# Routing on raw rows inside the last projection block of a fused encoder step

## The chip, the cores and the metric

The kernel runs on 1 core of one Trainium2 chip. The metric is the device time of one execution in microseconds; three runs of the kernel before took 517.83, 518.95 and 521.62 us, so the median is 518.95. A core has five engines with queues of their own, which meet only at semaphores: TensorE (PE in the rows, its weight loads PEld), VectorE (DVE), ScalarE (ACT), GpSimd (POOL) and SyncE (SP, which here only issues DMAs). ACT and POOL issue DMAs too.

## The reference, cut to what matters

One layer over 512 prompt tokens and 32 sample tokens of width 1024: norm, one input projection, a gated mixer beside a stick-breaking attention, an output projection with the residual, and then a mixture of experts. The part that the change touches:

```
h = yp + jnp.concatenate([gm, sb], axis=-1) @ w_out[l]
yp = h + hier_moe(rmsnorm(h, norm2_g[l]), *moe_args)

rmsnorm(x, g) = x * rsqrt(mean(x * x) + EPS) * g
lg    = xf @ w_router_group + b_router_group             # 4 group scores
g_sel = argmax(lg)                                       # one group of 4
le    = (xf @ w_router_expert + b_router_expert)[g_sel]  # 4 expert scores of that group
top_v, top_i = top_k(softmax(le), 2)                     # two experts per token
gates = softmax(lg)[g_sel] * top_v / sum(top_v)
y     = sum over the two of gate * (silu(x @ w_gate[e]) * (x @ w_up[e])) @ w_down[e]
```

There are 16 experts of inner width 256. All matrices are float32.

## The kernel before

Tokens are handled in five tiles (NT = 5): four of 128 rows and one of 32, the sample tile, which comes last. `x_sb` holds the rows x, and later h. The projections run as blocks of 512 output columns (`project(blk, after)`, L1469): a block has two halves, each half takes four 128-row pieces of the contraction for all five tiles, and `after[half](t)` puts other TensorE work between two tiles. Full tiles are computed in three float32r passes (L1465 to L1467) from a weight unit that was split in two parts: the high part by ACT, the low part (raw minus high) by DVE or POOL. The sample tile uses plain float32 (L1490). Blocks NB and NB + 1 are the output projection's two halves of columns; the last block, NB + 1, is weight units 12 and 13.

**Between the last projection block and the experts** the order of each queue is written out by hand:

- DVE adds the residual of each finished tile (`add_last`, L1225), normalises it into `xn2` (`norm_h`, L1208), and adds the router's bias (`logits`, L1219).
- ACT squares each finished row half with an accumulated sum (`square_h`, L866), copies transposed rows out of PSUM (`x2T_copy`, L874), and issues the store of normalised rows to the DRAM table `normed_tokens` (`store_normed`, L884).
- POOL makes the inverse root (L579 to L582) and the low part of expert unit 0 in four quarters (L586). The low parts of units 1 and 2 follow in `moe_gathers` (L592 to L596), ahead of the gathers in POOL's queue.
- TensorE transposes the normalised rows (`turn_normed`, L1675) and multiplies them with the padded router weights `wr_pad` (`router`, L1665): eight float32 products of 128 columns per tile. Three tiles' routers come after the projection's end.

The choice then runs on DVE as a chain (L1243 to L1339): in a chain, `link` makes each instruction wait for the one before. It finds the top group, the scores within the group, the two best experts, and the 0/1 selections `sel`. TensorE counts ranks by products with a triangular matrix (L1699 to L1706). A token's rank in its expert is its slot; an expert has CAP = 96 slots in a round. One-hot slot rows (`token_slots`) times token numbers (`slot_table`, L1709) give the token of each slot, which DVE writes to `idx_all`. POOL copies one column of it to `idx_cur` (L609) and issues an indirect DMA which gathers an expert's rows from `normed_tokens` into `xs` (L612). It waits for all stores of normalised rows before.

**The expert stage** (`moe`) takes three weight units of 1 MB per expert. Twelve raw buffers (NRAW) are filled from SP's queue ahead of use: units 0 to 5 once attention is done, unit 6 once unit 11 was used, unit 7 once unit 12 was used, units 8 to 11 once unit 13 was used, that is at the projection's end. Unit m from 12 on waits until units up to m - 12 have both parts made (`raw_free`, L409), and for the landing of the unit two before it (`few_in_flight`, L450). TensorE transposes the gathered rows (L1728), ACT and DVE split them, and the products follow.

After the experts POOL gathers each token's two result rows (L660) and DVE adds them with their gates (L1423).

## Time and profile before

| | |
|---|---|
| Median of three runs | 518.95 us |
| Profiled execution | 517.57 us |
| Its span, first to last instruction | 515.8 us |
| TensorE busy | 445.1 us, 86% |
| VectorE busy | 294.9 us, 57% |
| ScalarE busy | 251.2 us, 49% |
| GpSimd busy | 176.8 us, 34% |
| Mean granted TensorE clock | 0.944 |

The span is what the rows count from; the 1.8 us around it belong to the profiled execution's own time, and this execution is 1.4 us below the median of the runs. Busy shares are averages over stages with different limits, so a change in one stage is read from that stage. Of TensorE's clock 1.00 means 2.4 GHz and 0.50 means 1.2 GHz.

### The profile page before, as it was taken

The numbers are of one execution on the slowest core, as the hardware profiler recorded it, in microseconds if no ns is written. First come the engines' busy times: TensorE is split into PE (matmuls) and PEld (weight loads), VectorE is DVE, ScalarE is ACT, GpSimd is POOL, SyncE is SP. The second block draws the span as 40 slices with busy tenths as digits, with TensorE's granted clock in tenths as the row PEclk, the third lists the DMA queues.
The fourth block names the chain that finished last, engine by engine and source line by source line (L and its number), as shares of the span: only waits on it lengthen the run. The fifth ranks groups of instructions, "written<-read, shape, count | busy, mean of one in ns | idle before, by whom it ended". The sixth has DMA issues, their size and how long they took to land. (4 is left out here: it accounts for less than half of the span.)

```text
span 515.8 us, 7224 instructions
## 1 busy us (share of the span) xinstructions
PE 445.1 (86%) x2569; PEld 329.5 (64%) x2569; DVE 294.9 (57%) x442; ACT 251.2 (49%) x360; POOL 176.8 (34%) x179
## 2 busy tenths in 40 slices
PE   5999999999798999999999941799999999999400
PEld 4877877787586666667777841566666666666200
DVE  3535442354633645562333747358998998998236
ACT  4664333563424636462115521457877877877100
POOL 0384000514200000001003741137767767745270
PEclk9999999999979999999999985789999999999955
DMA  8872222222214000001695695269999999994376
GB/s 254 214 245 84 88 83 81 83 83 102 100 49 169 1 1 1 1 0 42 212 361 175 216 376 183 82 237 326 338 341 304 348 340 340 356 350 169 97 251 268
DMA packets 63445, 94.78 MB, mean 184 GB/s; under 512 B 10592, under 2 KB 43360, under 8 KB 63408
## 3 DMA queue, kind: packets, MB, share of 16 engines
q1 hardware_dynamic: 54336, 69.87, 41.6%
q0 software_dynamic: 5088, 17.89, 10.8%
q10 hardware_dynamic: 3984, 6.56, 3.5%
q8 instruction: 19, 0.31, 0.2%
q14 instruction: 18, 0.15, 0.1%
HBM read 81.27 MB, written 13.04 MB: 183 GB/s over the span
## 5 line engine op out<-in xcount | busy, mean ns | idle before, releaser
L1348 DVE TENSOR_TENSOR wlo<-raw,whi 128x2048 fp32r<-128x2048 f32 (+1 forms) x45 | 96.9, 2154 | 23.1 <-ACT whi L917 23.0
L1465 PE MATMUL bank<-whi,xT_hi 128*128 128x512 f32 x224 | 92.8, 414 | 2.7 <-DVE wlo L1015 2.1
L1466 PE MATMUL bank<-wlo,xT_hi 128*128 128x512 f32 x224 | 89.8, 401 | 0.0
L1467 PE MATMUL bank<-whi,xT_lo 128*128 128x512 f32 x224 | 89.6, 400 | 0.0
L917 ACT ACTIVATE whi<-raw 128x2048 fp32r<-128x2048 f32 x45 | 86.1, 1914 | 5.2 <-PE bank L1467 5.2
L622 POOL TENSOR_TENSOR wlo<-raw,whi 128x1024 fp32r<-128x1024 f32 x16 | 59.7, 3729 | 36.3 <-ACT whi L917 36.3
L1465 PE MATMUL bank<-whi,xsT_hi 128*96 128x512 f32 x128 | 53.8, 420 | 4.7 <-DVE xsT_lo L1354 3.5
L1465 PEld LDWEIGHTS bank<-whi,xT_hi 128*128 128x128 f32 x224 | 42.8, 191 | 14.3 <-issue 3.9
L1466 PE MATMUL bank<-wlo,xsT_hi 128*96 128x512 f32 x128 | 51.5, 403 | 0.0
L1467 PE MATMUL bank<-whi,xsT_lo 128*96 128x512 f32 x128 | 51.3, 401 | 0.0
L1467 PEld LDWEIGHTS bank<-whi,xT_lo 128*128 128x128 f32 x224 | 42.8, 191 | 10.5
L1466 PEld LDWEIGHTS bank<-wlo,xT_hi 128*128 128x128 f32 x224 | 43.0, 192 | 9.0
L1015 DVE SCALAR_TENSOR_TENSOR wlo<-raw,g_col,whi 128x512 fp32r<-128x512 f32 x40 | 27.9, 752 | 29.2 <-ACT whi L694 22.5
L576 POOL MEMSET wr_pad<- 128x1024 f32 x1 | 1.0, 954 | 100.1 <-issue 100.1
L513 POOL TENSOR_SCALAR ssq<-ssq 128x1 f32<-128x1 f32 (+3 forms) x25 | 5.0, 200 | 85.8 <-DVE ssq L1127 65.5
L694 ACT ACTIVATE whi<-raw,g_col 128x512 fp32r<-128x512 f32 x36 | 23.0, 710 | 23.2 <-PE bank L1490 19.5
L1465 PEld LDWEIGHTS bank<-whi,xsT_hi 128*96 128x96 f32 x128 | 21.2, 166 | 18.5 <-issue 7.0
L1465 PE MATMUL bank<-whi,aT_hi 128*96 128x512 f32 x64 | 26.1, 408 | 1.8 <-DVE aT_lo L1364 1.1
L609 POOL COPY idx_cur<-idx_all 96x1 int32<-96x1 int32 (+1 forms) x16 | 20.2, 1260 | 21.7 <-PE bank L1728 11.9
L1467 PEld LDWEIGHTS bank<-whi,xsT_lo 128*96 128x96 f32 x128 | 21.3, 166 | 9.5 <-issue 0.2
L1466 PEld LDWEIGHTS bank<-wlo,xsT_hi 128*96 128x96 f32 x128 | 21.3, 166 | 7.1
L515 POOL TENSOR_TENSOR rstd<-ssq,mhalf 128x1 f32<-128x1 f32 (+3 forms) x25 | 25.1, 1004 | 2.1
(223 smaller groups left out, 774.6 us busy)
## 6 DMA issues: line engine op xcount, KB each, us to landing
raw<-in_w_gate_dram SPq DMA_DIRECT2D x32, 512.0 KB, 6.1
raw<-in_w_up_dram SPq DMA_DIRECT2D x32, 512.0 KB, 7.5
raw<-in_w_down_dram SPq DMA_DIRECT2D x32, 512.0 KB, 6.8
raw<-in_w_in_dram SPq DMA_DIRECT2D x9, 1024.0 KB, 5.2
expert_rows<-yout POOLq DMA_DIRECT2D x16, 384.0 KB, 5.3
raw<-in_w_out_dram SPq DMA_DIRECT2D x4, 1024.0 KB, 5.1
x_sb<-in_x_prompt_dram SPq DMA_DIRECT2D x8, 256.0 KB, 6.1
normed_tokens<-xn ACTq DMA_DIRECT2D x4, 512.0 KB, 2.9
```

The lines of the kernel that those rows point to most:

```text
L513: link(pool.tensor_scalar(s, s, 1.0 / width, EPS, ALU.mult, ALU.add))
L515: return pool.tensor_tensor(dst, s, mhalf[0:s.shape[0], 0:n], ALU.pow)
L576: link(pool.memset(wr_pad[:, :, :], 0.0))
L609: pool.tensor_copy(idx_cur[p][:, :], idx_all[:, bass.ds(i, 1)]).then_inc(idx_cp, 1)
L622: pool.tensor_tensor(wlo[split][:, D:2 * D], eraw[slot][:, D:2 * D], whi[split][:, D:2 * D].bitcast(F32), ALU.subtract).then_inc(m_lo_pool, 1)
L694: ins = act.activation(whi[n % 2][:, c], raw[n % 3][:, c], ACT.Copy, scale=g1_col[:, kk:kk + 1])
L917: act.activation(whi[SPLIT_OF[m3]][:, :], eraw[slot][:, :], ACT.Copy).then_inc(m_hi, 1)
L1015: return dve.scalar_tensor_tensor(out=dst, in0=src, scalar=g1_col[:, kk:kk + 1], in1=hi.bitcast(F32), op0=ALU.mult, op1=ALU.subtract)
L1348: dve.tensor_tensor(wlo[SPLIT_OF[m3]][:, 0:n], eraw[slot][:, 0:n], whi[SPLIT_OF[m3]][:, 0:n].bitcast(F32), ALU.subtract).then_inc(m_lo, 1)
L1465: pe.matmul(acc, x_hi, w_hi, start=start, stop=False)
L1466: pe.matmul(acc, x_hi, w_lo, start=False, stop=False)
L1467: return pe.matmul(acc, x_lo, w_hi, start=False, stop=stop)
```

## The change

1. The router's products are made from the raw rows h, not the normalised ones. The factor 1/rms of a token is applied to the 20 scores afterwards (in `logits`), and the norm's gain is multiplied into the router weights `wr` once, early, by POOL. `wr_pad` goes; the products have 20 columns.
2. Since a raw row half is complete after the block before, the transposes and products of the first 512 columns run in the last block's first half, for all five tiles, and those of the second 512 in its second half. The second half takes the sample tile first (`LAST`), each tile's routing work stands inside the next tile's columns, and that of the last tile follows the projection.
3. POOL multiplies the rows with the gain (`times_g2`), ACT applies 1/rms and stores (`norm_store`). DVE's `norm_h` goes.
4. The expert choice is made over all 16 experts with the other groups pushed down by a large number; `sel` is bf16 and the rank products take the two choices apart. POOL makes the token numbers (`token_ids`). The slot products follow tile by tile behind ten small one-hot instructions, they accumulate both parts of a number, and DVE copies the first two experts' indices from PSUM straight to `idx_cur`.
5. The low parts of units 1 and 2 are made by DVE, the one before and the other after the first tokens' low parts. The places of the results and the gates are worked out after the indices as before. The first product of an expert waits for half of its tokens' parts, not all.
6. Buffers: `xn2` has five buffers, constants of the attention lie in its stack, and padded rows need no masks, since all products run over a tile's own rows.

```diff
+            pool.wait_ge(ld_wr, 16 * (NG + 1))
+            pool.wait_ge(ld_g2c, 16)
+            pool.tensor_tensor(wr[:, :, :], wr[:, :, :],
+                               g2_col[:, :].rearrange("p (k a) -> p k a", a=1).broadcast_to([P, KC, NE]), ALU.mult).then_inc(wr_ok, 1)
             pool.wait_ge(w_ok, 2 * NH)
             pool.wait_ge(pv_ok, NV)
...
+            def times_g2(t, half):
+                c = slice(half * CB, (half + 1) * CB)
+                pool.wait_ge(acc_free[t], 2 + half)
+                pool.tensor_tensor(xn2[t][0:rows[t], c], x_sb[0:rows[t], t, c], g2b[0:rows[t], c], ALU.mult).then_inc(hg_ok, 1)
...
+            for k, t in enumerate(LAST):
+                p = rows[t]
+                times_g2(t, 1)
+                pool.wait_ge(ssq2_ok, NT + k + 1)
+                link(pool.tensor_scalar(ssq[0:p, 3, t:t + 1], ssq[0:p, 3, t:t + 1], 1.0 / D, ssq[0:p, 2, t:t + 1], ALU.mult, ALU.add))
+                pool.tensor_tensor(rstd[0:p, 2, t:t + 1], ssq[0:p, 3, t:t + 1], mhalf[0:p, 0:1], ALU.pow).then_inc(rstd2_ok, 1)
+                if k < 4:
+                    c = slice(k * UNIT // 4, (k + 1) * UNIT // 4)
                     pool.wait_ge(m_hi, 1)
                     ins = pool.tensor_tensor(wlo[SPLIT_OF[0]][:, c], eraw[0][:, c], whi[SPLIT_OF[0]][:, c].bitcast(F32), ALU.subtract)
-                    if t == 3:
+                    if k == 3:
                         ins.then_inc(m_lo, 1)
...
+            pool.wait_ge(sel_ok, 2)
+            for t in range(NT):
+                token_ids(t)
...
-                for m in range(1 if isinstance(r, int) else 0, 3):
-                    pool.wait_ge(m_hi, u0 + m + 1)
...
+                    else:
+                        pool.wait_ge(idx_ok, s + 1)
+                        pool.sem_inc(idx_cp, 1)
                     pool.indirect_dma_start(xs[p][:, :], None, xn_dram[:, :],
...
+            def norm_store(k, t):
+
+                act.wait_ge(hg_ok, NT + k + 1)
+                act.wait_ge(rstd2_ok, k + 1)
+                act.activation(xn2[t][0:rows[t], :], xn2[t][0:rows[t], :], ACT.Copy, scale=rstd[0:rows[t], 2, t:t + 1]).then_inc(xn2_ok, 1)
+                act.wait_ge(xn2_ok, k + 1)
+                act.dma_start(xn_dram[tok(t), :], xn2[t][0:rows[t], :]).then_inc(xn_st, 16)
+
+            for t in range(NT):
+                x2T_copy(t, t, 0)
+                square_h(t, t, 0)
+            first_hi(1, slice(0, 3 * UNIT // 4))
             unit_used(act, U_IN + 2)
...
+            first_hi(0).then_inc(m_hi, 1)
+            first_hi(1, slice(3 * UNIT // 4, UNIT)).then_inc(m_hi, 1)
+            for k, t in enumerate(LAST):
+                square_h(NT + k, t, 1)
+                x2T_copy(NT + k, t, 1)
+                norm_store(k, t)
             unit_used(act, U_IN + 3)
-            first_hi(2)
+            first_hi(2).then_inc(m_hi, 1)
...
+            add_last(0)
+            for k in range(1, NT):
+                add_last(k)
+                logits(k - 1)
+            logits(NT - 1)
...
+            link(dve.tensor_tensor(of_group[:, :, :], of_group[:, :, :], wide(gtop, NG), ALU.subtract))
+            link(dve.tensor_tensor(m_all[0], e_all, of_group[:, :, :].rearrange("p t (g a) -> p t g a", a=1).broadcast_to([P, NT, NG, EPG]),
+                                   ALU.add))
             for c in range(2):
+                link(dve.tensor_reduce(v[c], masked[c][:, :, :], AX.X, ALU.max))
+                link(dve.tensor_tensor(firsts[:, :, :], masked[c][:, :, :], wide(v[c], E), ALU.is_equal))
+                link(dve.tensor_tensor(firsts[:, :, :], firsts[:, :, :], for_all(prio_e), ALU.mult))
+                link(dve.tensor_reduce(w[c], firsts[:, :, :], AX.X, ALU.max))
+                dve.tensor_tensor(sel[:, :, c, :], for_all(prio_e), wide(w[c], E), ALU.is_equal).then_inc(sel_ok, 1)
...
+            link(dve.tensor_tensor(ranks_of[:, :, :, :], rank, sel[:, :, :, :], ALU.mult))
+            link(dve.tensor_reduce(rank_of[:, :, :], ranks_of[:, :, :, :], AX.X, ALU.add))
+            for t in range(NT):
+                for c in range(2):
+                    ins = dve.tensor_scalar(onehot[0:rows[t], t, c, :], slot_no[0:rows[t], :], rank_of[0:rows[t], t, c:c + 1], None,
+                                            ALU.is_equal)
+                ins.then_inc(onehot_ok, 1)
+
+            dve.wait_ge(ids_mm, 1)
+            for i in range(2):
+                dve.tensor_copy(idx_cur[i][:, :], bank[5][0:CAP, i:i + 1]).then_inc(idx_ok, 1)
...
+                else:
+                    dve.wait_ge(m_lo, 1)
+                    lo(1, 1, 1)
+                    tokens_lo(0, 0)
+                    lo(2, 2, 2)
...
+            def router(n, t, half):
+
+                pe.wait_ge(x2T_ok, n + 1)
+                if n == 0:
+                    pe.wait_ge(wr_ok, 1)
+                elif n > NT:
+                    pe.wait_ge(lg_ok, n - NT)
+                for k in range(UK):
+                    mm = pe.matmul(bank[7][0:rows[t], t * LG:t * LG + NE], x2T[:, k, 0:rows[t]], wr[:, UK * half + k, :],
+                                   start=(n == 0 and k == 0), stop=(half == 1 and k == UK - 1), skip_group_check=True)
                 mm.then_inc(r_mm, 1)
...
+            def first_columns(i, k):
+
+                if k == 1:
+                    turn_rows(i, 0)
+                elif k == UK - 1:
+                    router(i, i, 0)
+
+            def last_columns(i, k):
+
+                if i >= 1 and k == 1:
+                    turn_rows(LAST[i - 1], 1)
+                elif i >= 1 and k == UK - 1:
+                    router(NT + i - 1, LAST[i - 1], 1)
+
+            project(NB + 1, (first_columns, last_columns), LAST)
+            turn_rows(LAST[-1], 1)
+            router(2 * NT - 1, LAST[-1], 1)
+            ranks()
...
                 def gate_up(i, p, half, m3, unit):
                     s = s0 + i
+                    pe.wait_ge(xsT_lo_ok, 2 * s + half + 1)
                     if half == 0:
-                        pe.wait_ge(xsT_lo_ok, 2 * s + 2)
```

## Rows read from the trace of the kernel before

**Rows 1.** Busy time in stretches; behind the engines the granted clock, DMA share, GB/s.

```profile
273.50:290.00 16.50, 16.17 (x116) 13.28 (x113) 9.31 (x8) 11.69 (x22) 9.27 (x16) 1.00 0.40 137
290.00:317.70 27.70, 13.43 (x118) 12.13 (x118) 18.03 (x56) 7.59 (x14) 11.25 (x7) 0.81 0.89 307
350.00:450.00 100.00, 98.63 (x483) 68.48 (x482) 88.52 (x82) 77.81 (x85) 73.42 (x43) 1.00 1.05 337
```

**Rows 2.** Timeline, TensorE from the last block on: start, us taken, instructions, idle before.

```profile
261.04 0.50 PE L1465 MATMUL bank<-whi,xT_hi 128*128 128x512 f32 x1
...
273.45 0.50 PE L1465 MATMUL bank<-whi,xT_hi 128*128 128x512 f32 x1
...
286.17 1.95 PE L1672 MATMUL bank<-wr_pad,x2T 128*128 128x128 f32 x16
287.95 1.04 PE L1437 MATMUL bank<-ident,xn 128*128 128x128 f32 x8
288.92 1.08 PE L1490 MATMUL bank<-raw,xT_s 128*32 128x128 f32 x32
...
303.84 1.99 PE L1672 MATMUL bank<-wr_pad,x2T 128*32 128x128 f32 x16 [0.36 <-DVE lg L1223]
...
322.09 1.54 PE L1728 MATMUL bank<-ident,xs 96*128 96x96 f32 x8 [6.13 <-DMA xs<-normed_tokens,idx_cur]
324.81 0.74 PE L1465 MATMUL bank<-whi,xsT_hi 128*96 128x512 f32 x1 [1.17 <-DVE xsT_lo L1354]
```

**Rows 3.** Weight loads grouped by shape, 236 to 325 us: busy us, mean ns.

```profile
L1672 PEld LDWEIGHTS bank<-wr_pad,x2T 128*128 128x128 f32 x48 | 5.7, 191 | 1.6 <-ACT x2T L882 1.5
...
L1672 PEld LDWEIGHTS bank<-wr_pad,x2T 128*32 128x32 f32 x16 | 1.7, 114 | 0.7 <-issue 0.6
```

**Rows 4.** Timeline, VectorE from the projection's end to the first experts.

```profile
286.37 0.69 DVE L1229 TENSOR_TENSOR x_sb<-x_sb,bank 128x512 f32<-128x512 f32 x1 [0.67 <-PE bank L1467]
...
293.92 5.53 DVE L1216 SCALAR_TENSOR_TENSOR xn_late<-x_sb,rstd,g2b 32x1024 f32<-32x1024 f32 x1 [1.28 <-POOL rstd L515]
...
305.87 0.17 DVE L1223 TENSOR_TENSOR lg<-bank,br 32x20 f32<-32x20 f32 x1 [2.18 <-PE bank L1672]
...
311.82 0.24 DVE L1283 TENSOR_TENSOR selb<-r,valid 128x80 bf16<-128x80 f32 x1
...
313.70 1.23 DVE L1301 TENSOR_TENSOR onehot<-slot_no,rank_of 128x480 bf16<-128x480 bf16 x2
...
331.30 2.29 DVE L1348 TENSOR_TENSOR wlo<-raw,whi 128x2048 fp32r<-128x2048 f32 x1 [6.54 <-ACT whi L917]
```

**Rows 5.** Timeline, GpSimd in the same stretch.

```profile
289.40 0.55 POOL L515 TENSOR_TENSOR rstd<-ssq,mhalf 128x1 f32<-128x1 f32 x1
289.92 1.27 POOL L586 TENSOR_TENSOR wlo<-raw,whi 128x512 fp32r<-128x512 f32 x1
...
293.86 4.50 POOL L595 TENSOR_TENSOR wlo<-raw,whi 128x2048 fp32r<-128x2048 f32 x1
...
317.74 1.08 POOL L612 DMA_INDIRECT xs<-normed_tokens,idx_cur  x1 [0.90 <-POOL idx_cur L609]
```

**Rows 6.** Timeline, ScalarE: high parts of units 0 and 1, and a copy of transposed rows.

```profile
273.58 3.72 ACT L860 ACTIVATE whi<-raw 128x2048 fp32r<-128x2048 f32 x2 [10.43 <-PE bank L1490]
...
293.27 0.59 ACT L882 ACTIVATE x2T<-bank 128x512 f32<-128x512 f32 x1
```

**Rows 7.** Costliest groups of the page: GpSimd's low parts in the expert stage.

```profile
L622 POOL TENSOR_TENSOR wlo<-raw,whi 128x1024 fp32r<-128x1024 f32 x16 | 59.7, 3729 | 36.3 <-ACT whi L917 36.3
```

**Rows 8.** DMA issues by window, us to landing: first gather; normed rows among unit loads.

```profile
xs<-normed_tokens,idx_cur POOLq DMA_INDIRECT x1, 4.3
...
normed_tokens<-xn ACTq DMA_DIRECT2D x1, 512.0 KB, 7.3
```

**Rows 9.** The gathers as a tile, expert stage: time from issue to landing over all.

```profile
DMA to landing us min/median/max: 4.0/7.1/8.5
```

**Rows 10.** Waits of SP's own queue: what it waited for, us in total, times, longest.

```profile
SPq L455 <- DMA raw<-in_w_up_dram: 50.4, 20, 5.1
```

More of the change, by code:

```diff
@@ L601, in moe_gathers @@
-                pool.wait_ge(idx_ok, r + 1)
-                pool.sem_inc(pool_tick, 1)
+                first = isinstance(r, int)
+                if not first:
+                    for m in range(3):
+                        pool.wait_ge(m_hi, u0 + m + 1)
+                        pool.sem_inc(pool_tick, 1)
+                        lo_unit(m, slice(0, UNIT)).then_inc(m_lo, 1)
+                    pool.sem_inc(m_lo_pool, 1)
+                    pool.wait_ge(idx_ok, r + 3)
+                    pool.sem_inc(pool_tick, 1)
@@ L884, in store_normed @@
[L884 to L898 removed]
+                return act.activation(whi[SPLIT_OF[m]][:, c], eraw[m][:, c], ACT.Copy)
@@ new lines, in _ @@
+            for c in range(2):
+                ins = dve.scalar_tensor_tensor(out=rk[c][:, :], in0=rd[c][:, :], scalar=float(SLOTS - CAP), in1=rank_c[c],
+                                               op0=ALU.mult, op1=ALU.add)
+            link(ins)
+            for c in range(2):
+                ins = dve.scalar_tensor_tensor(out=rk[c][:, :], in0=top[:, TOP_W0 + c, :], scalar=-float(CAP), in1=rk[c][:, :],
+                                               op0=ALU.mult, op1=ALU.add)
+            link(ins)
@@ L1467, in three_passes, with project @@
                 return pe.matmul(acc, x_lo, w_hi, start=False, stop=stop)
-            def project(blk, after):
+            def project(blk, after, order=range(NT)):
                 for half in range(2):
@@ L1477, in project @@
                         pe.wait_ge(sbT_lo, NV)
-                    for t in range(NT):
+                    for i, t in enumerate(order if half else range(NT)):
                         if blk == 0:
@@ L1704, in _, with turn_rows @@
-            for t in range(NT):
-                mm = pe.matmul(bank[7][:, NT * E:(NT + 1) * E], onesb[:, :], selb[:, t, :], start=(t == 0), stop=(t == NT - 1))
-            mm.then_inc(rank_ok, 1)
-            def slot_table(r):
-                pe.wait_ge(onehot_ok, r + 1)
-                for m in range(2 * NT):
-                    mm = pe.matmul(bank[4][0:CAP, 0:2 * E], onehot[:, m, :], ids_of[:, m, :], start=(m == 0), stop=(m == 2 * NT - 1))
-                mm.then_inc(ids_mm, 1)
+            def turn_rows(t, half):
+                pe.wait_ge(acc_free[t], 2 + half)
+                if half:
+                    pe.wait_ge(ssq2_ok, NT)
+                turn4(bank[5 + half], x_sb[0:rows[t], t, half * CB:(half + 1) * CB], rows[t], x2_tr)
@@ new lines, in ranks @@
+            def ranks():
+                for c in range(2):
+                    pe.wait_ge(sel_ok, c + 1)
+                    for t in range(NT):
+                        dst = bank[4][:, t * E:(t + 1) * E]
+                        for t2 in range(t):
+                            pe.matmul(dst, onesb[0:rows[t2], :], sel[0:rows[t2], t2, c, :], start=False, stop=False, skip_group_check=True)
+                        pe.matmul(dst, before[0:rows[t], :], sel[0:rows[t], t, c, :], start=(c == 0 and t == 0), stop=True,
+                                  skip_group_check=True)
+                    for t in range(NT):
+                        mm = pe.matmul(bank[4][:, COUNT0:COUNT0 + E], onesb[0:rows[t], :], sel[0:rows[t], t, c, :], start=False,
+                                       stop=True, skip_group_check=True)
+                mm.then_inc(rank_ok, 1)
@@ new lines, in slot_rows @@
+            def slot_rows(t, p, first):
+                for c in range(2):
+                    for a in range(2):
+                        mm = pe.matmul(bank[5][0:CAP, 0:E], onehot[0:p, t, c, :], ids_of[0:p, t, c, a, :],
+                                       start=(first and c == 0 and a == 0), stop=True, skip_group_check=True)
+                return mm
+            def first_columns(i, k):
[3 more added lines that the diff above has]
+                    router(i, i, 0)
@@ L1716, in moe @@
+            mm.then_inc(ids_mm, 1)
             def moe(r):
                 s0, u0 = E * r, 3 * E * r
-                slot_table(r)
+                if not isinstance(r, int):
+                    pe.wait_ge(onehot_ok, r + NT)
+                    for t in range(NT):
+                        mm = slot_rows(t, rows[t], t == 0)
+                    mm.then_inc(ids_mm, 1)
                 def turn_tokens(i, p, n):
                     s = s0 + i
+                    if isinstance(s, int) and s < 1:
+                        pe.wait_ge(idx_ok, 3)
```

404 lines of the change are left out of this document (157 added, 247 removed).

## The prediction, made before the changed kernel ran

> **What bounds the kernel now.** I read the stretches first, then each engine's timeline between the last projection block and the experts, then the DMA landings. In the expert stage TensorE is busy for 98.63 of 100 us [rows 1], so there its work sets the time, with the 16 DMA engines full beside it (share 1.05). Up to 290.00 it is busy too (16.17 of 16.50). Between them lies a hole: from 290.00 to 317.70 it works 13.43 of 27.70 us [rows 1], at a mean granted clock of 0.81, and the first expert product begins only at 324.81 [rows 2]. The projection's last product, the sample tile's, began at 288.92 and ends near 289.9. So 34.9 us pass from the projection's end to the experts, and nothing but a chain of small steps sets them: 16.1 us to the last scores, written at 306.04; 11.7 us of choice up to the first gather at 317.74; 4.35 us for its rows; 2.7 us to split them [rows 2, 4, 5]. What shortens this chain moves all that follows, as long as weights come in time.
>
> **Part 1, the projection's end moves back.** The two halves of the last block begin at 261.04 and 273.45 [rows 2], so a half costs 12.4 us of its own. The second half also held two pairs of transposes and a router, 4.1 us, which is why it ended at 289.9. After the change the routing work stands inside both halves. Four transposes are half of the eight between 287.95 and 288.92: 0.45 to 0.5 us. A router half is 8 records in place of 16. Before, 16 took 1.78 us (286.17 to 287.95 [rows 2]), 0.11 each, with 128 columns moving. Now 20 columns move, so the question is whether the weight load sets the pace. The load of 128 columns is shown with 191 ns, that of 32 with 114 ns [rows 3]: 77 ns for 96 columns, so 0.10 us for 128. I take 0.11 us a record, 0.89 us a router half, with bounds 0.3 (the products alone, by columns, with a little overhead) and 1.04 (0.13 a record). A full tile costs 1.34 us in each half, the sample tile some 0.5.
>
> The Trainium skill, page "TensorE: Matmul & The Clock Gate", section "LDWEIGHTS (loading the stationary operand)", gives the load time as columns over 1.2 in ns, 107 ns here. By it the cut from 128 to 20 columns saves nothing, against this part of the change; by the moving columns alone the sum would come out some 3 us lower.
>
> First half: 12.4 + 4 x 1.34 + 0.5 = 18.3 us, so it ends at 279.3. In the second the sample comes first (0.5 extra), and up to the last column three transposes and two routers of full tiles are added (1.35 + 1.8). One stall joins: ACT works in order, and at 279.3 it still has the last square (0.8 us), then three quarters of unit 1 (1.4), unit 0 and the rest of unit 1 (3.72 for both whole units, so 2.3 more [rows 6]), the sample's second square (0.8) and only then the copy of its transposed rows (0.3, 0.59 for a full one [rows 6]). That is about 5.9 us after the half's end, where TensorE wants it at 4.6: **1.3 us of stall**. Queued behind that wait on TensorE is the whole projection. So the second half ends at 279.3 + 12.4 + 0.5 + 3.15 + 1.3 = **296.7**, 6.8 us later than before. SP's loads of units 8 to 11, which wait for that end, move by the same 6.8 us; I cost that under part 4.
>
> **Part 2, the last scores.** Before, three routers, two transposes and a normalisation that took 5.53 us [rows 4] instead of a fraction stood between projection and scores; that one ran beside POOL's 4.50 us low part [rows 5], and the change removes both. Now there remain: the last tile's addition (0.9 from the last product, as 0.69 in [rows 4] and the wait), transposes 0.5, ACT's copy 0.6 with a short wait for its square, the last router half 0.9, the score 0.2, and semaphores: **3.6 us**. The inverse root comes at the same time: after the addition POOL does a multiply of 512 columns (1.27 as L586), a small sum (0.2) and the power (0.55) [rows 5], so 3.1. Scores at 300.3 against 306.04: **5.7 gained**. The new multiplies cost nothing in the block: POOL needs 2 x 1.27 + 0.55 + 0.4 = 3.5 us a tile, TensorE 4.1 to 4.4. Without that cover TensorE waits, which is a rival below.
>
> **Part 3, the choice.** Before, 25 chained instructions took the 6.0 us from the last score (305.87 + 0.17) to `selb` (311.82 + 0.24) [rows 4], 0.24 each. Now 17 stand there, 11 of them on 80 elements (0.27): 4.3 us. The rank products of the first choice hide behind the second; the second's 20 take 0.8 with the hand-over. Two wide instructions follow, 0.7. The one-hot instructions were two for 1.23 us [rows 4]; ten small ones cost about 1.0, but four slot products per tile follow each pair at the low clock, 20 of them, so 2.1 for both. The index copies go straight to `idx_cur`: 0.2, and POOL's copy with the 0.90 us wait behind it [rows 5] becomes one wait, 0.5. Sum 8.7 against 11.7: **3.0 gained**, first gather at 309.0. POOL's five `token_ids` (about 0.3 each) run beside the rank step, before their products need them.
>
> **Part 4, the gather.** It lands 4.35 us after its start now, since the DMA engines have just become free; the same gathers among loads take 7.1 in the median, 4.0 to 8.5 at the ends [rows 8, 9]. After the change units 8 to 12 leave from 296.7 on, and 5 MB of loads with 2 MB of row stores at some 340 GB/s [rows 1] last until about 316, so the gather runs among them. I take 7.1: **2.8 lost**. It also waits for the last store: root at 299.8, ACT's multiply 1.1, issue at 301.4, landing 7.3 later as that of 292.90 did [rows 8], at 308.7, just in time. Splitting: the first product now waits for half the parts, 2.15 instead of 2.72 us, **0.6 gained**. DVE makes unit 1's low part (2.29 [rows 4]) before the tokens' parts; with the bookkeeping after the indices (3.2 + 1.0) it is done 6.7 us after them, while the tokens' high parts need 0.5 + 7.1 + 1.5 = 9.1, so it hides in the gather. With a gather of 4.3 it would be 0.4 late. Unit 2's follows with 10 us in hand.
>
> **Part 5, what follows.** First expert product at 309.0 + 7.1 + 2.15 = 318.3 against 324.81: 6.5 earlier. Loads from unit 15 on are released by use of earlier units, so they move with the experts; units 13 and 14, held now by DVE's low parts, leave at about 315 and 320 and land before unit 15 starts. Later SP waits for landings (50.4 us on one line [rows 10]), but ACT never waits for a raw unit. So the shift stays. The small load of the gain and POOL's scaling of `wr` lie in the idle time of the attention.
>
> **Sum:** 517.57 - 6.5 = 511.1 for the profiled execution; the median stands 1.4 higher, so **512.5**.
>
> **Rivals.** *All cheap* (16%): router halves at the lower bound, no ACT stall and a gather of 4.3 us. Then 3 + 1.3 + 2.8 more are gained less what other queues take back, about 506. The weight-load rows speak against the first, ACT's order against the second.
>
> *The DMA traffic eats it* (18%): the loads pushed back by 6.8 us delay the last store and then the gather. With a landing of 10 us for the store and 8.5 for the gather the rows arrive at 320.5, the first product is at 322.7, and the time is 516.9. For it: share 0.89 already in that stretch [rows 1]. Against: the stores took at most 7.3.
>
> *GpSimd paces the second half, slower* (10%): each tile's multiply, root and quarter stand in front of ACT's `norm_store`, and this in front of the next square and copy, for which TensorE waits. At 3.5 us a tile this is hidden. In the expert stage the same kind of instruction takes 3729 ns for 1024 columns [rows 7] against 1.27 for 512: 1.46 times; that gives 4.9 us a tile, 3.5 lost in all, 516. At twice the cost it is 6.4 a tile, 2.3 over TensorE for four tiles and 1.5 behind, 10.7 lost: 523.2. It decides from 1.7 times on, 5.6 us a tile. Against: in this block DVE's additions read one operand from PSUM, and POOL's 1.27 was measured beside such ones.
>
> The Trainium skill, page "SBUF — State Buffer", section "Who interferes with whom", says that a DVE instruction with two SBUF inputs and a GpSimd one reading SBUF lock each other out for a whole instruction; the 5.53 us agree. By it this rival does not happen, as no such DVE instruction is left in the block.
>
> *The change does less than it says*: a stage of the choice still waits on unit 2's high part or the exponentials; they are asked for only after the indices, so this is inside the forecast.
>
> **Chances.** Forecast 56%, with its own range of 509.5 to 516. The range with the others: all cheap reaches down to 507 within it, the traffic and a mild GpSimd case up to 519. What a measurement tells from no change is 1%, 5.2 us: faster below 513.8. About two thirds of the forecast's case and all of the cheap one lie there, together 0.55; the rest of it, the traffic and most of the GpSimd case lie within 1%, 0.37; 0.08 slower.
>
> **What would show it.** Steps: last projection product at 296.7; the records of the 20-column products 0.11 us apart; scores done at 300.3; the selection 4.3 us later; first gather at 309.0 and its landing 7 us on; the idle time before the sample's second router; POOL 3.5 us a tile; first expert product at 318.3; TensorE as busy as before afterwards. It is wrong if the gather waits for a store, if TensorE stops within the second half at each tile, or if TensorE waits for weights in the experts.

## The result, and the profile after

The changed kernel takes **511.44 us** (median of 4 runs, 510.6 to 512.2) against 518.41 us (4 runs, 517.83 to 521.62): 7 us less. The ratio over all fast runs is 0.9856, 95% interval 0.9826 to 0.9886 (that of the two medians alone is 0.9866). The profiled execution took 510.60 us, its span is 509.0 (before 515.8), at a mean granted clock of 0.943.

TensorE's timeline after, at the places that [rows 2] show of before (start, us taken, engine, line, work, idle time before it):

```profile
258.19 0.51 PE L1475 MATMUL bank<-whi,xT_hi 128*128 128x512 f32 x1
...
261.51 0.96 PE L1692 MATMUL bank<-wr,x2T 128*128 128x20 f32 x8
262.32 0.48 PE L1475 MATMUL bank<-whi,xT_hi 128*128 128x512 f32 x1
...
276.37 1.04 PE L1500 MATMUL bank<-raw,xT_s 128*32 128x128 f32 x29
...
281.16 0.43 PE L1692 MATMUL bank<-wr,x2T 128*32 128x20 f32 x8 [0.21 <-ACT x2T L905]
281.52 0.50 PE L1475 MATMUL bank<-whi,xT_hi 128*128 128x512 f32 x1
...
293.26 0.96 PE L1692 MATMUL bank<-wr,x2T 128*128 128x20 f32 x8
...
303.57 1.86 PE L1715 MATMUL bank<-ids_of,onehot 128*96 128x16 bf16 x20 [1.28 <-DVE onehot L1300]
313.55 1.51 PE L1761 MATMUL bank<-ident,xs 96*128 96x96 f32 x8 [8.12 <-DMA xs<-normed_tokens,idx_cur]
315.59 0.74 PE L1475 MATMUL bank<-whi,xsT_hi 128*96 128x512 f32 x1 [0.53 <-DVE xsT_lo L1356]
```

Read it against the block's own start, because that start has moved too: 258.19 after, 261.04 before [rows 2]. From it to the first expert product there were 63.8 us (261.04 to 324.81) and there are 57.4 (258.19 to 315.59): 6.4 less. The remaining 2.85 us lie ahead of anything that the prediction looked at.

VectorE's choice, as in [rows 4]; GpSimd and ScalarE follow, as in [rows 5] and [rows 6]:

```profile
296.65 0.24 DVE L1253 SCALAR_TENSOR_TENSOR lg<-bank,rstd,br 128x20 f32<-128x20 f32 x1 [2.15 <-PE bank L1692]
...
301.00 0.24 DVE L1288 TENSOR_TENSOR sel<-prio_e,top 128x80 bf16<-128x80 f32 x1
302.40 0.32 DVE L1296 TENSOR_TENSOR ranks_of<-bank,sel 128x160 f32<-128x160 f32 x1 [1.16 <-PE bank L1707]
...
303.11 1.62 DVE L1300 TENSOR_SCALAR onehot<-slot_no,rank_of 128x96 bf16<-128x96 bf16 x10
305.47 0.22 DVE L1306 CAST idx_cur<-bank 96x1 int32<-96x1 f32 x2 [0.73 <-PE bank L1715]
```

```profile
286.63 1.30 POOL L575 TENSOR_TENSOR xn<-x_sb,g2b 128x512 f32<-128x512 f32 x1
287.97 0.26 POOL L593 TENSOR_SCALAR ssq<-ssq 128x1 f32<-128x1 f32 x1
288.31 0.57 POOL L594 TENSOR_TENSOR rstd<-ssq,mhalf 128x1 f32<-128x1 f32 x1
288.83 1.31 POOL L598 TENSOR_TENSOR wlo<-raw,whi 128x512 fp32r<-128x512 f32 x1
...
306.54 1.06 POOL L636 DMA_INDIRECT xs<-normed_tokens,idx_cur  x1 [3.90 <-DVE idx_all L1307]
```

```profile
276.55 3.79 ACT L888 ACTIVATE whi<-raw 128x1536 fp32r<-128x1536 f32 x3
...
280.86 0.25 ACT L905 ACTIVATE x2T<-bank 128x128 f32<-128x128 f32 x1
...
297.66 0.33 ACTq L913 DMA_DIRECT2D normed_tokens<-xn  x1
```

The last scores are written at 296.89, the choice ends at 301.24, the first gather starts at 306.54 and its rows are on TensorE 7.0 us later. GpSimd's tile is 1.30 + 0.26 + 0.57 + 1.31 = 3.4 us: nothing stretched it.

Two stretches, columns as in [rows 1]:

```profile
294.00:306.50 12.50, 5.78 (x74) 4.92 (x74) 7.62 (x43) 4.89 (x8) 3.39 (x8) 0.62 0.96 341
...
350.00:450.00 100.00, 97.69 (x482) 69.14 (x481) 93.16 (x83) 77.44 (x84) 70.96 (x42) 1.00 1.05 326
```

The choice still leaves TensorE more than half idle (busy 5.78 of 12.50 us), with the DMA engines nearly full beside it (share 0.96). In the expert stage TensorE is nearly as busy as in [rows 1], 97.69 of 100 us.

Then the experts. Both kernels at their second expert (its first product and the transposes for the third), before and after:

```profile
334.57 0.62 PE L1465 MATMUL bank<-whi,xsT_hi 128*96 128x512 f32 x1 [1.87 <-DVE xsT_lo L1354]
...
341.93 0.82 PE L1728 MATMUL bank<-ident,xs 96*128 96x96 f32 x8
```

```profile
325.91 0.47 PE L1475 MATMUL bank<-whi,xsT_hi 128*96 128x512 f32 x1 [1.50 <-DVE xsT_lo L1356]
...
331.69 0.82 PE L1761 MATMUL bank<-ident,xs 96*128 96x96 f32 x8
```

The third expert's transposes come 10.2 us earlier, though the first product came 9.2 earlier: before, TensorE stood still for 1.87 us and came back to a lower granted clock (mean 0.82 from 334.57 to 344.00, its first eight products 0.62 us each); after, it stood 1.50 and the clock stayed at 1.00 (325.91 to 334.00). This is no chance of one profile: in all five profiles of kernels without the whole change (before, and experiments 1, 2, 9 and 11) several products of the second expert take about 0.63 us, in none of the nine with it. Experiment 2, which has only the moved low parts, still shows it, so another part of the change removed it; which one was not tried. But the last product of all ends at 475.03 instead of 484.10, 9.1 earlier: over 1 us is given back. ScalarE's waits between 290 and 490 us show waits for weights that the first profile of the kernel before does not have (waited for, us in total, times, longest):

```profile
ACT whi L943 <- DMA raw<-in_w_up_dram: 3.1, 2, 2.3
ACT whi L943 <- DMA raw<-in_w_down_dram: 1.9, 3, 1.3
```

And the tail. GpSimd's last store of expert rows and its first gather of results, before and after:

```profile
485.38 0.51 POOL L629 DMA_DIRECT2D expert_rows<-yout  x1 [3.75 <-DVE yout L1372]
491.03 1.02 POOL L660 DMA_INDIRECT raw<-expert_rows,pos_y  x1 [5.13 <-issue]
```

```profile
476.31 0.52 POOL L653 DMA_DIRECT2D expert_rows<-yout  x1 [3.78 <-DVE yout L1374]
484.33 1.01 POOL L688 DMA_INDIRECT raw<-expert_rows,pos_y  x1 [7.49 <-issue]
```

From TensorE's end to the span's end: 515.8 - 484.1 = 31.7 us before, 509.0 - 475.0 = 34.0 after.

**The span's account:** ahead of the block -2.85, block to first expert product -6.35, experts +0.15 (159.3 to 159.4 us, which hides -1.0 at the second expert and a little over +1 later), tail +2.3. Sum -6.8, and 515.8 - 509.0 = 6.8.

### The profile page after: what moved, and what is told of

It is laid out like the page before. It is cut to its first block and busy times, and to the rows that moved or that the text cites. A ratio compares the mean times of both kernels' runs of the same rounds, so it can differ in the third digit from the quotient of the medians.

```text
span 509.0 us, 7334 instructions
## 1 busy us (share of the span) xinstructions
PE 439.7 (86%) x2599; PEld 328.6 (65%) x2599; DVE 285.5 (56%) x434; ACT 256.4 (50%) x366; POOL 181.6 (36%) x186
## 5 line engine op out<-in xcount | busy, mean ns | idle before, releaser
L1350 DVE TENSOR_TENSOR wlo<-raw,whi 128x2048 fp32r<-128x2048 f32 (+1 forms) x47 | 103.7, 2207 | 20.1 <-ACT whi L943 20.0
L943 ACT ACTIVATE whi<-raw 128x2048 fp32r<-128x2048 f32 x45 | 86.2, 1915 | 10.5 <-PE bank L1477 5.5
L1476 PE MATMUL bank<-wlo,xT_hi 128*128 128x512 f32 x224 | 88.6, 395 | 0.0
L1475 PE MATMUL bank<-whi,xsT_hi 128*96 128x512 f32 x128 | 52.5, 411 | 2.7 <-DVE xsT_lo L1356 2.7
L722 ACT ACTIVATE whi<-raw,g_col 128x512 fp32r<-128x512 f32 x36 | 23.0, 710 | 22.8 <-PE bank L1500 19.2
L1477 PE MATMUL bank<-whi,aT_lo 128*96 128x512 f32 x64 | 25.2, 394 | 0.0
L1476 PE MATMUL bank<-wlo,aT_hi 128*96 128x512 f32 x64 | 25.1, 393 | 0.0
```

What stands on the lines that cost most here:

```text
L722: ins = act.activation(whi[n % 2][:, c], raw[n % 3][:, c], ACT.Copy, scale=g1_col[:, kk:kk + 1])
L943: act.activation(whi[SPLIT_OF[m3]][:, :], eraw[slot][:, :], ACT.Copy).then_inc(m_hi, 1)
L1350: dve.tensor_tensor(wlo[SPLIT_OF[m3]][:, 0:n], eraw[slot][:, 0:n], whi[SPLIT_OF[m3]][:, 0:n].bitcast(F32), ALU.subtract).then_inc(m_lo, 1)
L1475: pe.matmul(acc, x_hi, w_hi, start=start, stop=False)
L1476: pe.matmul(acc, x_hi, w_lo, start=False, stop=False)
L1477: return pe.matmul(acc, x_lo, w_hi, start=False, stop=stop)
```

## The experiments

Each ratio is to the kernel before, timed on the same chip.

**1. The kernel before once more** (no edit), to see whether the block's start moves by itself.

> The kernel before, unchanged, to see how much of the difference between the two traces is there without the change: in the changed kernel's trace the last projection block begins 2.9 us earlier, though no step ahead of it was meant to get faster. If that is the spread of one execution against another, this trace's block begins anywhere between 258 and 261. If it belongs to the change (other addresses of the attention's constants, fewer GpSimd constants), it begins within 0.3 us of 261.0 again.

520.99 us in one run; the block's first product is at 260.73, within 0.3 us of 261.0 as expected for that case. So nearly all of the 2.85 us belongs to the change. A single profile can still be off here: that of experiment 5 begins its block at 259.48 and the late one of experiment 10 at 263.88, while the other six with the change and without a pad begin it at 258.0 to 258.7. In the profile of this run ScalarE waited 4.6 us for weights in the experts, in the first profile of the same kernel not at all: the kernel before stands close to that limit itself.

**2. Before, with VectorE making the low parts of units 1 and 2** after the choice, instead of GpSimd beside it.

```diff
-                for m in range(1 if isinstance(r, int) else 0, 3):
+                for m in range(3 if isinstance(r, int) else 0, 3):
...
+                    lo(1, 1, 1)
+                    tokens_lo(0, 0)
+                    lo(2, 2, 2)
```

> The kernel before with one part of the change alone: the low parts of units 1 and 2 are made by VectorE around the first tokens' parts, not by GpSimd ahead of the gathers. Theory (a lock between the engines sat on the chain): the normalisation of the sample tile, 5.53 us before, takes about 1.3, the last scores come 4.2 us earlier, unit 1's part is late by 0.4 on VectorE, and the time falls by 3.7 us, to some 514.7. Rival (GpSimd's parts were off the path): less than 1 us.

513.5 us (6 runs), ratio 0.9896 (0.9852 to 0.9940), a little below the 514.7 expected. Its rows of VectorE and TensorE:

```profile
293.85 1.27 DVE L1216 SCALAR_TENSOR_TENSOR xn_late<-x_sb,rstd,g2b 32x1024 f32<-32x1024 f32 x1 [1.28 <-POOL rstd L515]
```

```profile
320.58 0.74 PE L1472 MATMUL bank<-whi,xsT_hi 128*96 128x512 f32 x1 [1.17 <-DVE xsT_lo L1354]
```

The normalisation that took 5.53 us [rows 4] beside GpSimd's 4.50 us part takes 1.27 without it: 4.26 us, and the first expert product is 4.2 us earlier. This small part alone gives most of the gain: 1.04% of 1.44%. Its second expert still has the stretch at the lower clock:

```profile
331.31 0.63 PE L1474 MATMUL bank<-whi,xsT_lo 128*96 128x512 f32 x1
```

**3. After, with those two low parts back on GpSimd.**

```diff
+            for m in (1, 2):
+                pool.wait_ge(m_hi, m + 1)
+                lo_unit(m, slice(0, UNIT)).then_inc(m_lo, 1)
             pool.wait_ge(sel_ok, 2)
...
-                    dve.wait_ge(m_lo, 1)
-                    lo(1, 1, 1)
                     tokens_lo(0, 0)
-                    lo(2, 2, 2)
```

> The changed kernel with that part undone: units 1 and 2 on GpSimd again, ahead of the token numbers. Theory: GpSimd's two 4.5 us instructions start at about 296.4, just as the choice starts on VectorE, whose instructions with two SBUF inputs wait them out; token numbers come after 305.4; so the first gather moves from 306.5 to 312 or later and the time rises by 4 to 7 us. Rival (only the queue order counts, no lock): the gather moves by 2 us and the time by 1 to 2.

517.84 us (10 runs), ratio 1.0009 (0.9973 to 1.0045): the whole gain is gone. VectorE, then GpSimd:

```profile
296.95 3.77 DVE L1280 TENSOR_TENSOR of_group<-lg,top 128x20 f32<-128x20 f32 x1
300.76 4.42 DVE L1281 TENSOR_TENSOR of_group<-of_group,prio_g 128x20 f32<-128x20 f32 x1
```

```profile
296.17 8.96 POOL L604 TENSOR_TENSOR wlo<-raw,whi 128x2048 fp32r<-128x2048 f32 x2
```

Two instructions on 20 elements take 3.77 and 4.42 us where their like takes 0.18: each ends with one of GpSimd's two parts. The first gather starts at 314.18 instead of 306.54, 7.6 us later. With GpSimd at work there the rest of the change comes to nothing in the sum, though this run too has the early start of the block (258.01). That does not make the rest worthless: both of GpSimd's parts now fall on the choice and hold it up by 7.8 us, while in the kernel before one of them held up the normalisation by 4.3 and the other one instruction of the choice by about 0.5 (0.73 us at 306.28).

**4. After, with half the columns of the weights of units 36 to 47** (the last four experts). The other half of their buffers keeps old data, and the engines do the same work on it.

```diff
+                    load_gate_up(i, half, slot, FF // 2 if isinstance(m, int) and m >= 3 * (E - BODY) else FF)
...
+                    load_down(i, slot, D // 2 if isinstance(m, int) and m >= 3 * (E - BODY) else D)
```

> The changed kernel, but the weight loads of units 36 to 47 (the last four experts' share) bring only half of their columns, so these experts compute with old data in the other half. Instructions of the engines are the same. Theory (weights come too late at the end of the changed kernel, since its experts start 9 us earlier and their loads 3 us later): ScalarE's waits for raw units of the last two experts go and the time falls by 2 to 2.5 us. Rival (the loss of 2.5 us over the experts is TensorE's or ScalarE's own): no change.

511.63 us (10 runs), ratio 0.9831 (0.9801 to 0.9862), which the timing cannot tell from the change's own 0.9856. In the profile ScalarE no longer waits for a load, and TensorE ends at 473.77 instead of 475.03: between these two profiles late weights make 1.3 us, less than the 2 to 2.5 expected. Waits are not a cost by themselves: the profile of experiment 8 has 3.9 us of them, and its experts take 158.0 us (318.65 to 476.67), as long as here without any (158.1), against 159.4 in the change.

**5. After, with the loads of units 8 and up held back until the indices are there**, to free the first gather of traffic.

```diff
                             unit_used(sp_, U_ALL - 3 + min(m - 6, 2))
+                            if m >= 8:
+                                sp_.wait_ge(idx_ok, 1)
```

> The changed kernel, with one more wait on the load queue: units 8 to 11 (and so all after them) leave only once the first expert's indices are there, 12 us later than now. Theory: the first gather meets no loads and lands after 4.3 us, not 6.9, so the first expert product comes 2.6 us earlier; but the DMA engines are then full from 306 to the end and cannot make up 12 us, so the weights of the last experts come late and the time rises by 7 to 10 us. Rival (TensorE alone sets the expert stage): the time falls by 2.6 us.

520.87 us (10 runs), ratio 1.0019 (0.9981 to 1.0057). TensorE, then ScalarE's waits:

```profile
317.01 1.51 PE L1763 MATMUL bank<-ident,xs 96*128 96x96 f32 x8 [10.28 <-DMA xs<-normed_tokens,idx_cur]
```

```profile
ACT whi L945 <- DMA raw<-in_w_up_dram: 12.7, 6, 3.0
...
ACT whi L945 <- DMA raw<-in_w_down_dram: 6.5, 5, 1.8
```

The gather did not get its 4.3 us: it took 9.2 (307.84 to 317.01), and SyncE issues the held loads from 307.02 on, beside it. That half of the expectation was my mistake in the design. The other half came as expected: 19.2 us of waits for weights, and TensorE ends 10.5 us later than in the change, of which 1.3 lie ahead of the block in this profile (259.48) and have nothing to do with the held loads.

**6. After, with raw and output buffers changed in place, so that units 8 and 9 wait for the same earlier unit as unit 7** and no longer for the block's last: the opposite of 5.

```diff
-        yout = [sb(f"yout{i}", [CAP, D]) for i in range(2)]
         late = [sb(f"raw{i}", [P, UNIT]) for i in range(9, NRAW)]
+        late = [late[0], late[2], late[1]]
+        yout = [sb(f"yout{i}", [CAP, D]) for i in range(2)]
...
-                            unit_used(sp_, U_ALL - 3 + min(m - 6, 2))
+                            unit_used(sp_, U_ALL - 3 + (0, 1, 1, 1, 2, 2)[m - 6])
```

> The changed kernel with two of its raw buffers laid over the halves of the transposed activations that are free once the last block's first half is done; units 8 and 9 then leave at 276 to 280, in a stretch where the DMA share is 0.3, and not at 293. Theory: less traffic at the gather (landing 4.3 to 6 us in place of 6.9) and 6 us more in hand for the weights at the end; the time falls by 3 to 5 us, to 506.5 to 508.5. Rival (the end does not wait for weights): 0 to 2.6 us, from the gather alone.

**507.39 us** (4 runs), ratio 0.9782 (0.9740 to 0.9824), as expected. TensorE:

```profile
310.83 1.51 PE L1762 MATMUL bank<-ident,xs 96*128 96x96 f32 x8 [5.57 <-DMA xs<-normed_tokens,idx_cur]
312.88 0.74 PE L1476 MATMUL bank<-whi,xsT_hi 128*96 128x512 f32 x1 [0.53 <-DVE xsT_lo L1357]
```

The gather starts at 306.37, as in the change, and lands in 4.5 us instead of 7.0; ScalarE's waits for weights fall from 5.0 to 1.1 us. First product 2.7 us and TensorE's end (470.78) 4.25 us earlier, so 1.5 us are won in the experts.

**7. The edits of 4 and 6 together.**

> Both: early loads of units 8 and 9, and half the columns in units 36 to 47. Theory: with the early loads no weight is late any more, so this is within 1 us of the early loads alone. If it is faster by more, weights still set the end.

507.14 us (4 runs), ratio 0.9777 (0.9735 to 0.9819), TensorE's end 470.79: with the early loads nothing is left for shorter weights to give.

**8 and 9. Where xT_hi lies.** What the kernels differ in ahead of the block, apart from their code, is the place of their buffers. A pad of 32 bytes per partition in each kernel puts it to the test.

```diff
         mix = ExitStack()
+        pad = sb("pad", [P, 8])
         xT_hi = sb("xT_hi", [P, KC, SEQ], F32R, stack=mix)
```

> The changed kernel with one unused buffer of 32 bytes per partition ahead of xT_hi, so that xT_hi, xT_lo and every buffer behind them (raw3 to raw11, xsT_hi, xsT_lo among them) lie 32 bytes further on. Theory 'place': in the changed kernel the products of the projections that load xT_hi or xT_lo follow each other every 229.2 ns, in the kernel before every 233.2 ns, because the change took 1,824 bytes away ahead of xT_hi and moved it from a place 32 bytes beyond a multiple of 64 (102,496) onto a multiple of 64 (100,672). Then here the pitch is 233.2 ns again, 672 such products by 4.0 ns are 2.7 us, the last projection block's high part starts at 261.0 instead of 258.2, and the ratio to the kernel before is 0.990 to 0.992 instead of 0.986. Rival 'the router moved out': the 2.8 us ahead of the block come from something else that the change moved. Then the pitch stays at 229.2 ns and the time at 511.4 us.

> The kernel before with one unused buffer of 32 bytes per partition ahead of xT_hi: xT_hi lies at 102,528, a multiple of 64. Nothing else differs. Theory 'place': the pitch falls from 233.2 to 229.2 ns, the last block's high part starts at 258.3 to 258.5, and the time falls by 2 to 3 us, ratio 0.994 to 0.996 (the experts' products, 232.0 to 231.3 ns in the two kernels, would give under 2 us more where TensorE sets their time, and they wait for ScalarE's high parts). Rival 'the router moved out': no change, 1.000.

After with the pad: 513.01 us (4 runs), ratio 0.9900 (0.9866 to 0.9934). Before with the pad: 515.15 us (6 runs), ratio 0.9931 (0.9908 to 0.9955). First and last of 47 products of the projections that follow each other without a break, in the kernel before, after, after with the pad, before with the pad (the last two with the block's start):

```profile
236.57 0.39 PE L1466 MATMUL bank<-wlo,xT_hi 128*128 128x512 f32 x1
...
247.30 0.40 PE L1467 MATMUL bank<-whi,xT_lo 128*128 128x512 f32 x1
```

```profile
246.31 0.40 PE L1476 MATMUL bank<-wlo,xT_hi 128*128 128x512 f32 x1
...
256.85 0.40 PE L1477 MATMUL bank<-whi,xT_lo 128*128 128x512 f32 x1
```

```profile
236.45 0.39 PE L1477 MATMUL bank<-wlo,xT_hi 128*128 128x512 f32 x1
...
247.18 0.40 PE L1478 MATMUL bank<-whi,xT_lo 128*128 128x512 f32 x1
...
260.93 0.50 PE L1476 MATMUL bank<-whi,xT_hi 128*128 128x512 f32 x1
```

```profile
246.75 0.40 PE L1467 MATMUL bank<-wlo,xT_hi 128*128 128x512 f32 x1
...
257.20 0.39 PE L1468 MATMUL bank<-whi,xT_lo 128*128 128x512 f32 x1
...
258.53 0.50 PE L1466 MATMUL bank<-whi,xT_hi 128*128 128x512 f32 x1
```

By 46 steps: 10.73 us, 10.54, 10.73, 10.45, so 233, 229, 233 and 227 ns a product. The pad takes the gain ahead of the block from the one kernel (block at 260.93) and gives it to the other (258.53). The rival, that the moved routing did it, falls both times. The time of 9 fell by 3.6 us, somewhat over the 2 to 3 expected, and its pitch by 6 ns instead of 4. Those 46 steps are a sample: over all steps of the projections at the higher clock (567 to 597 in each trace) the means are 233.1, 229.6, 233.1 and 228.2 ns. For the 576 products ahead of the block that gives 2.0 and 2.8 us, where the pad moved the block by 2.74 and 2.51. So the pitch of these products explains the second shift and about three quarters of the first; where the pad's other 0.7 us arise was not looked for.

**10, 11 and 12. GpSimd's branches in the other order.** At the end of its program the further rounds stood first and the usual case's fetch behind them; here the fetch stands first. 10 and 12 are the version of 6 with this edit, 11 is the kernel before with it.

```diff
-            with pool.If(more != 0):
+            with pool.If(more == 0):
+                fetch(SLOTS)
+            with pool.Else():
                 with pool.Fori(1, ROUNDS) as r:
                     moe_gathers(r)
                 fetch(ROUNDS * SLOTS)
-            with pool.Else():
-                fetch(SLOTS)
```

> The version of e6_early_loads with the two branches at the end of GpSimd's program exchanged: the results' fetch for the usual case (no further round) stands first, right behind the jump, and the further rounds stand behind it. Theory 'code fetch': the 7.5 us without work between GpSimd's last store of expert_rows and its first result gather in every kernel with the change (5.0 to 5.1 in the kernels before it) hold the loading of instructions that lie far off behind the unused branch, and the change moved those; here the code follows on, the idle time falls to 3 to 5 us, and the time falls from 507.4 to 503 to 505.5 us. Rival 'the transfer': the idle time is the last store's own landing and the flag's read, which no order of the code changes; then it stays at 7.5 us and the time at 507.4 us, within 0.5.

> The kernel before with the two branches at the end of GpSimd's program exchanged as in e10_fetch_first: the usual case's fetch stands first. Theory 'the change moved far code': the kernel before idles 5.1 us between GpSimd's last store of expert_rows and its first result gather, as much as e10_fetch_first (4.9) and less than every kernel with the change (7.5), so its fetch branch was already at hand after the jump; the idle time stays at 4.8 to 5.2 us and the ratio at 0.999 to 1.001. Rival 'shorter in any kernel': code that follows on is worth 2.5 us here too, idle 2.5 us, ratio 0.995.

> e10_fetch_first once more, in more rounds, since its times lay far apart (504.5 to 510.4 us) and its profiled run was late from 140 us on, in stretches at a low granted clock. If exchanging the branches is worth what its idle row shows (7.5 to 4.9 us), the median is 504.8 to 505.5 us, ratio 0.973 to 0.975, against 507.4 us and 0.978 for e6_early_loads; the idle row is 4.9 us again. If the gain is given back later (the gathers' transfers end together whatever the start), the median stays at 507 us.

10: 506.41 us (4 runs, 504.46 to 510.39), ratio 0.9753 (0.9717 to 0.9788). 12: **506.36 us** (6 runs, 505.06 to 508.59), ratio 0.9758 (0.9728 to 0.9788). 11: 518.77 us, ratio 0.9999 (0.9980 to 1.0019). GpSimd's first result gather in 12, then in 11:

```profile
478.46 1.01 POOL L689 DMA_INDIRECT raw<-expert_rows,pos_y  x1 [4.94 <-issue]
```

```profile
491.64 1.02 POOL L660 DMA_INDIRECT raw<-expert_rows,pos_y  x1 [4.58 <-issue]
```

The idle time falls from 7.5 to 4.9 us where the change is in, and from 5.13 to 4.58 in the kernel before, a little under the bound that I gave. So the transfer of the last store, which lands 3.4 to 3.8 us after its issue in all of them, does not set the 7.5, and the order of the code does in good part. Of the 2.6 us less only 1.5 reach the end: from the last store to VectorE's last additions it is 25.6 us in version 6 and 24.1 in 12. The medians show 1.0, with overlapping intervals; 10 missed the 503 to 505.5 and 12 the 504.8 to 505.5 that I expected.

The traces show what goes on in that gap. A DMA queue of kind "instruction" moves packets in it, here in the change from 475 to 485.5 us and in 12 from 472 to 479.5 (packets, MB, share):

```profile
q14 instruction: 5, 0.04, 1.3%
```

```profile
q14 instruction: 3, 0.02, 1.1%
```

They come in rounds 2.2 to 2.7 us apart. In the change there are four, at about 477.2, 479.6, 482.0 and 484.2, and the gather starts at 484.33; version 6 and experiment 8 have four as well. The kernel before has three (486.0, 488.5, 490.9, gather at 491.03), and 11 and 12 have two (487.2 and 489.6; 473.9 and 476.3). So the change's gap holds one round of instruction loading more than the gap before it did, and it is longer by about one round, 2.4 us. This supports the theory 'code fetch'. The count is not the whole of it: 11 and 12 have a round fewer than the kernel before, and their gaps are only 0.2 to 0.6 us shorter than its. That the packets are GpSimd's is inferred from these times, and whether the place or the length of its code adds the round was not tried apart.

## Why the prediction was right

The forecast case came about: 512.5 us with 507 to 519 given, 511.44 measured, and the sum's own 511.1 for the profiled execution stands beside 510.6. Its steps, counted from the block's start so that the 2.85 us stay out (add them to the times of after):

- **Part 1** gave 296.7 for the projection's end; 293.26 + 2.85 = 296.1. The first half came as worked out (18.2 us to the sample's second products at 276.37, against 18.3). A router half takes 0.81 us (261.51 to 262.32), 0.10 a record with 20 columns moving, and 0.91 at most: the weight load sets the pace, not the moving columns. The sample tile shows it: its eight records load 32 columns instead of 128, move the same 20, and take 0.36 us (281.16 to 281.52). By the Trainium skill, page "TensorE: Matmul & The Clock Gate", section "LDWEIGHTS (loading the stationary operand)", the time of a load goes by its columns alone, which is 107 ns for 128. The trace agrees, with 101 to 114 ns a record. The ScalarE stall was mis-sized: 1.3 predicted, 0.21 in the row for 281.16 (under 0.4 with the hand-over). The working put the last square of the first half after that half's end; it ran before, so ScalarE's 3.79 us of high parts began 0.2 us after it and ended at 280.34, early enough for the copy at 280.86. Other small delays made up about half of what this saved.
- **Part 2**, scores at 300.3: 296.89 + 2.85 = 299.7. The step of 3.6 us after the last product measured 3.6 (293.26 to 296.89).
- **Part 3**, the choice, 8.7: measured 9.65 (296.89 to 306.54). The chain to the selection is 4.35 as said, but the ranks' hand-over took 1.16 instead of 0.8, one-hots and slots 2.35 instead of 2.1, and GpSimd began 0.85 after the indices instead of 0.5. The slip is in hand-overs between engines, each a few tenths short. The part's own terms also add up to 8.6, not 8.7.
- **Part 4**, landing 7.1 and splitting 2.15: 7.0 and 2.04. Experiment 6 shows the cause that was named: the same gather with the loads moved ahead lands in 4.5. By the trace the last store was issued at 297.66 and landed 6.4 us later, before the gather at 306.54, so the gather did not wait for it; the rival of the DMA traffic wanted 10 us for the store and 8.5 for the gather. *All cheap* wanted a router half of 0.3 us and a gather of 4.3; only its missing stall came.
- **GpSimd's pace**, the slower rival: 3.4 us a tile against 3.5 predicted. It does not stretch as in [rows 7]. Experiment 3 shows what happens when VectorE instructions on two operands in SBUF stand beside such a part: 3.77 and 4.42 us in place of 0.18. By the Trainium skill, page "SBUF — State Buffer", section "Who interferes with whom", a VectorE instruction with two inputs in SBUF contends with a GpSimd one that reads SBUF, and the lock is exclusive. Both durations agree with that.
- **Part 5** said "So the shift stays" and that "ACT never waits for a raw unit". The first holds by its net (experts +0.15), the second failed: 5.0 us of waits, of which 1.3 reach TensorE's end by the pair of profiles in experiment 4. I read the wait rows of one profile as a margin; experiment 1 shows 4.6 us of such waits in the kernel before itself.
- **Slips that changed nothing.** Of the selection's 17 instructions 12, not 11, work on 80 elements. The stall's listed terms add up to 5.6 us, not 5.9. The GpSimd rival's 4.9 and 6.4 us a tile hold about 1.3 us of fixed parts where the forecast's 3.5 holds 0.95. And the chances say that most of the GpSimd case lies within 1%, but the 0.37 given there is already used up by the rest of the forecast (0.19) and the traffic (0.18).

**What the sum left out** is what this case teaches: four terms beside the hole, two of each sign. The earlier start of the block gave -2.85, of which the pad takes 2.74 back; the second expert at the higher clock gave -1.0, the later experts a little over +1 (late weights, as far as experiment 4 shows it), the tail +2.3. They come to about zero, so the number was closer than the working deserved: that part was luck. With the place taken out (experiment 8, 513.01 us) the whole change is no faster than its smallest part done alone (experiment 2, 513.5 us): against it the rest saves 1.9 us up to the first expert product (318.65 against 320.58) and 1.7 in the experts (158.0 against 159.7), and the tail, longer by 3.2 (31.3 us in experiment 2, 34.5 in experiment 8), takes nearly all of it back.

## What to carry to other kernels

Where a serial chain of small VectorE instructions sets the time, look first at what GpSimd does beside it: moving two instructions gave most of what a rewritten chain gave. Bound the weights' supply before counting a shift as kept, and ask which loads collide with the chain's one urgent transfer; here moving them ahead of it was worth another 4 us, holding them behind it cost 9. And when buffers move, compare the pitch of the products that did not change: here 32 bytes in the list of buffers sped up one kernel and slowed down the other in a stage that the diff never touches.

## What the runs showed of the hardware that I had not expected

- **The place of the loaded operand.** The pitch of fp32r products of 512 columns at the higher clock is 233 ns with xT_hi at byte 102,496 of the partition (32 beyond a multiple of 64), 229 at 100,672 (a multiple of 64, not of 128), 227 at 102,528 (a multiple of 128) and 233 at 100,704. The figures are of 46 steps each; the means over the whole trace are 233.1, 229.6, 228.2 and 233.1, in the same order. xT_lo and all later buffers moved with it, so which of them matters was not told apart; in the expert stage the pitch went from 232.0 to 231.4 only.
- **A gather's landing** follows what leaves with it: 4.3 to 4.6 us with few loads beside it (DMA share while it was under way 0.42 in the kernel before, 0.57 in experiment 6), 6.7 us at a share of 0.72 (experiment 3), 7.0 to 7.2 among loads under way (1.08 in the change), 9.2 when held loads left at the same moment.
- **The last branch of GpSimd** cost 4.6 to 7.5 us before its first instruction, by code order and kernel, with the same store ahead of it. Packets on a DMA queue of kind "instruction" fall into this time: two rounds at 4.6 and 4.9 us, three at 5.1, four at 7.5.
